# One transformer layer on one core: the gate weights stacked into one operand, and a head's values taken in one block of matmuls ahead of the next head's transposes

## What is computed

```python
proj = x @ w_in
qa, ka, va, qk_m, vm, om, gates = jnp.split(proj, SPLITS, axis=-1)
att = dilated_attention(heads(qa, 8), heads(ka, 8), heads(va, 8), rel_table)
...
ig = (gates[..., :4] + ig_b).transpose(0, 2, 1)      # 4 heads x 512
fg = (gates[..., 4:] + fg_b).transpose(0, 2, 1)
h = mlstm(heads(qm, 4), heads(km, 4), heads(vm, 4), ig, fg)
...
# memory_attention
kv = (mem @ wkv).reshape(B, L, 2, 4, 256)
k, v = kv[:, :, 0], kv[:, :, 1]
```

## Time and profile before

| | us |
|---|---|
| three runs | 1163.87, 1164.14, 1164.82 (median 1164.14) |
| the profiled execution | 1164.95 |
| its span in the trace | 1163.0 |
| PE busy | 1150.1 (99% of the span), 5490 matmuls |
| PE weight loads | 958.7 (82%) |
| DVE / ACT / POOL busy | 573.1 / 422.2 / 32.7 |
| granted PE clock | 0.999 of 2.4 GHz |

### The profile page before, as it was taken

One profiled execution on the slowest core, in us unless ns is written; L12 is line 12 of the kernel. 1 busy time (PEld: TensorE's weight loads), 2 busy tenths in 40 slices (PEclk: granted clock), 3 DMA queues, 4 the chain that ended last, 5 costly groups with the idle time before them and its releaser, 6 DMA issues.

```text
span 1163.0 us, 14755 instructions
## 1 busy us (share of the span) xinstructions
PE 1150.1 (99%) x5490; PEld 958.7 (82%) x5490; DVE 573.1 (49%) x930; ACT 422.2 (36%) x688; POOL 32.7 (3%) x49
## 2 busy tenths in 40 slices
PE   9999999999999999999999999999999999999997
PEld 8888888888888777888798888789888888888886
DVE  3533333343328588765884864456433333343325
ACT  4412212233225377643463454444221222233222
POOL 3000000000001011000000000000000000000000
PEclk9999999999999999999999999999999999999999
DMA  7532222232222222242243241232322222232211
GB/s 282 212 104 95 90 105 93 90 122 95 91 90 73 91 75 82 81 152 85 73 160 112 93 149 67 73 109 91 127 92 107 90 95 104 90 123 95 91 36 73
DMA packets 33563, 120.85 MB, mean 104 GB/s; under 512 B 3900, under 2 KB 3916, under 8 KB 33264
## 3 DMA queue, kind: packets, MB, share of 16 engines
q1 hardware_dynamic: 30528, 109.07, 27.3%
q0 software_dynamic: 2992, 11.19, 2.8%
HBM read 118.13 MB, written 2.11 MB: 103 GB/s over the span
## 4 chain that ended last, share of the span: by engine, by line
PE 97%; DVE 2%; ACT 1%; issue 0%; DVEq 0%; POOL 0%; POOLq 0%
PE ps L446 31%; PE ps L448 30%; PE ps L447 30%; PE ps L463 1%; PE ps L668 1%; PE ps L689 1%; PE ps L740 1%; PE ps L756 1%; PE ps L661 0%; PE ps L597 0%; PE ps L660 0%; DVE lg L1536 0%; PE ps L850 0%; DVE qs L1493 0%; DVE lg L1544 0%
## 5 line engine op out<-in xcount | busy, mean ns | idle before, releaser
L1336 DVE TENSOR_TENSOR wlo<-raw,whi 128x1024 fp32r<-128x1024 f32 x196 | 240.0, 1228 | 373.0 <-ACT whi L911 371.9
L446 PE MATMUL ps<-xth,whi 128*128 128x512 f32 (+1 forms) x924 | 355.0, 384 | 0.0
L448 PE MATMUL ps<-xth,wlo 128*128 128x512 f32 (+1 forms) x924 | 353.0, 382 | 0.0
L447 PE MATMUL ps<-xtl,whi 128*128 128x512 f32 (+1 forms) x924 | 352.9, 382 | 0.0
L911 ACT ACTIVATE whi<-raw 128x1024 fp32r<-128x1024 f32 (+1 forms) x204 | 207.1, 1037 | 152.1 <-PE ps L448 142.8
L448 PEld LDWEIGHTS ps<-xth,wlo 128*128 128x128 f32 x924 | 173.7, 188 | 34.1
L447 PEld LDWEIGHTS ps<-xtl,whi 128*128 128x128 f32 x924 | 173.8, 188 | 32.9
L446 PEld LDWEIGHTS ps<-xth,whi 128*128 128x128 f32 x924 | 173.8, 188 | 32.4
L446 PE MATMUL ps<-whi,hhi 128*128 128x512 f32 x480 | 187.8, 391 | 0.0
L448 PE MATMUL ps<-whi,hlo 128*128 128x512 f32 x480 | 186.9, 389 | 0.0
L447 PE MATMUL ps<-wlo,hhi 128*128 128x512 f32 x480 | 186.8, 389 | 0.0
(11 more groups left out here) (186 smaller groups left out, 997.2 us busy)
## 6 DMA issues: line engine op xcount, KB each, us to landing
raw<-in_units SPq DMA_DIRECT2D x204, 512.0 KB, 3.3
gb<-in_ln_g POOLq DMA_DIRECT2D x4, 512.0 KB, 3.9
gb<-in_ln_b POOLq DMA_DIRECT2D x4, 512.0 KB, 5.4
xn<-in_x POOLq DMA_DIRECT2D x4, 512.0 KB, 12.0
wb<-in_bias_by_key POOLq DMA_DIRECT2D x8, 256.0 KB, 3.0
out<-xn SPq DMA_DIRECT2D x8, 256.0 KB, 2.1
gsp<-g_rows POOLq DMA_DIRECT2D x1, 1024.0 KB, 4.8
memn<-in_mem_cols POOLq DMA_DIRECT2D x1, 1024.0 KB, 8.1
```

The costliest lines, as they stand in the source:

```text
L446: mm(dst, lh, rh, start=start, stop=False)
L447: mm(dst, lh, rl, start=False, stop=False)
L448: return mm(dst, ll, rh, start=False, stop=stop)
L1336: v.tensor_tensor(wlo[c % SPL][:, :], raw[c % RAW][:, :], whi[c % SPL][:, :].bitcast(F32), ALU.subtract).then_inc(lo_done, 1)
```

## The change

- The gate weights are one operand `wg` of 100 columns: high parts in columns 0 to 35, zeros, low parts in columns 64 to 99. Two matmuls for each slice (against the high and the low part of x) replace three; rows 64 and up of the result hold the products of the low weights. ACT copies two more blocks of 4x512 out (`r_e`, `r_a`), and DVE adds them where it added a bias alone. `wg` lies in the memory of `vx`, so POOL now fills `wg` with zeros at the start, and `vx` with ones once the gate rows are done.
- The probabilities of a whole head stand in `ph` and `pl`. `values(h)` is one block of 8 matmuls (512, 512, 384, 384, 256, 256, 128, 128 columns) in step 4h + 6, ahead of that step's transposes; the part in step 4h + 4 is gone.
- DVE writes the first two `kl` ahead of the split of weight unit `U_QK + 5`.
- `mem_key(0)` waits for the first half of `mtl`, and for the second after 12 matmuls.

```diff
             for k in range(KT):
-                last = three(ps[1][0:GW, :], wg_hi[:, k, :], wg_lo[:, k, :], xh[:, k, :], xl[:, k, :], k == 0, k == KT - 1)
+                mm(ps[1][0:64 + GW, :], wg[:, k, :], xh[:, k, :], start=k == 0, stop=False)
+                last = mm(ps[1][0:64 + GW, :], wg[:, k, :], xl[:, k, :], start=False, stop=k == KT - 1)
             last.then_inc(grow_ready, 1)
...
-            def values(h, part):
-
-                i0 = 2 * part
-                pe.wait_ge(p_lo_done, NB * h + i0 + 2)
...
+            def values(h):
+
+                pe.wait_ge(p_lo_done, NB * h + NB)
...
+                for j in range(NB):
+                    cols = slice(4 * j * P, (3 * j + NB) * P)
+                    for p in (ph, pl):
+                        last = mm(ps[4 + h % 2][:, j * P:], vs[j][:, h, :], p[:, cols],
+                                  start=j == 0 and p is ph, stop=j == NB - 1 and p is pl)
                 last.then_inc(pv_done, 1)
...
             def attention(n):
+                if n % NB == 2 and n > NB:
+                    values(n // NB - 1)
                 if 2 <= n < NA + 2:
                     transpose_p(n - 2)
                 if n < NA:
                     logits(n)
-                if n >= NB and n % 2 == 0:
-                    values(n // NB - 1, n // 2 % 2)
...
                 if t == 0:
-                    pe.wait_ge(mlo_done, 2)
                     pe.wait_ge(pj_ev, evacuated(G_C2 + 3))
...
-                cols_part(U_XK + t, ps[6 + t % 2][:, 0:MB * P], mth, mtl, 0, KT)
+                for half in range(2):
+                    if t == 0:
+                        pe.wait_ge(mlo_done, half + 1)
+                    cols_part(U_XK + t, ps[6 + t % 2][:, 0:MB * P], mth, mtl, 4 * half, 4 * half + 4)
...
             fn(r_f[:, :], ps[1][32:GW, :], ACT.Copy).then_inc(f_ready, 1)
+            fn(r_e[:, :], ps[1][96:64 + GW, :], ACT.Copy).then_inc(f_ready, 1)
+            fn(r_a[:, :], ps[1][64:64 + MH, :], ACT.Copy).then_inc(f_ready, 1)
...
-            split(U_QK + 5)
             k_lo(0, 0)
             k_lo(0, 1)
+            split(U_QK + 5)
```

More of the change, by code:

```diff
@@ L205, in macaron_layer @@
         pt = [at(f"pt{s}", [P, S], ar + (64 + 2 * s) * KB) for s in range(PTS)]
[L206 to L209, removed]
+        ph = at("ph", [P, 13 * P], ar + 64 * KB, F32R)
+        pl = at("pl", [P, 13 * P], ar + 64 * KB + 13 * P * 4, F32R)
         ob = [at(f"ob{s}", [P, NB, P], ar + (74 + 2 * s if s < 2 else 52 + 2 * s) * KB) for s in range(MH)]
@@ L213, in macaron_layer @@
         grow = at("grow", [MH, S], ar + 82 * KB + NB * MH * (P + 1) * 4)
-        wg_hi = at("wg_hi", [P, KT, GW], ar + 82 * KB + NB * MH * (P + 1) * 4, F32R)
-        wg_lo = at("wg_lo", [P, KT, GW], ar + 82 * KB + NB * MH * (P + 1) * 4 + KT * GW * 4, F32R)
+        wg = at("wg", [P, KT, 64 + GW], ar + 82 * KB, F32R)
         mth = at("mth", [P, KT, MB * P], ar + 32 * KB, F32R)
@@ L330, in transposed, with prob_blocks @@
         def transposed(n):
[L332 to L340, removed]
+            return ps[2 + n % 2][:, 0:(n % NB + 1) * P].rearrange("p (j c) -> p j c", c=P)
+        def prob_blocks(p, i):
+            return p[:, i * P:(4 * i + 1) * P].rearrange("p (j c) -> p j c", c=P)[:, 0:3 * i + 1:3, :]
         block = ctx.enter_context(nc.Block())
@@ L372, in _ @@
                                     base=0, pattern=[[-1, P]], channel_multiplier=1).then_inc(pool_ok, 1)
-            nc.gpsimd.memset(vx[:, :, :, :], 1.0).then_inc(pool_ok, 1)
+            nc.gpsimd.memset(wg[:, :, :].bitcast(F32), 0.0).then_inc(pool_ok, 1)
             pool.wait_ge(lo_done, KT - 2)
@@ L412, in _ @@
             bias_masked(1)
+            pool.wait_ge(grow_ready, 1)
+            nc.gpsimd.memset(vx[:, :, :, :], 1.0).then_inc(pool_ok, 1)
             pool.wait_ge(rows_done, 1)
@@ L426, in _ @@
                                     channel_multiplier=-1).then_inc(gdiag_done, 1)
-            pool.wait_ge(pv_done, 2 * AH)
+            pool.wait_ge(pv_done, AH)
             pool.dma_start(memn[:, :, :], mem_cols).then_inc(mem_in, 16)
@@ L670, in transpose_p @@
                 last.then_inc(tr_done, 1)
-            def values(h, part):
-                i0 = 2 * part
-                pe.wait_ge(p_lo_done, NB * h + i0 + 2)
-                if part == 0 and h == 1:
+            def values(h):
+                pe.wait_ge(p_lo_done, NB * h + NB)
+                if h == 1:
                     pe.wait_ge(acol_done, 1)
                     pe.wait_ge(emin_done, 1)
-                if part == 0 and h >= 2:
+                if h >= 2:
                     pe.wait_ge(att_out, h - 1)
[L681 to L689, removed]
+                for j in range(NB):
[3 more added lines that the diff above has]
+                                  start=j == 0 and p is ph, stop=j == NB - 1 and p is pl)
                 last.then_inc(pv_done, 1)
@@ L747, in numerators @@
                     pe.wait_ge(pj_ev, evacuated(G_VM + NB - 1))
-                    pe.wait_ge(pool_ok, 2)
+                    pe.wait_ge(pool_ok, 3)
                     pe.wait_ge(att_out, AH)
@@ L974, in ffn_up @@
                     act.wait_ge(small_in, 16 * SMALL)
-                    fn(wg_hi[:, :, :], wg_raw[:, :, :], ACT.Copy).then_inc(wg_hi_done, 1)
+                    act.wait_ge(pool_ok, 2)
+                    fn(wg[:, :, 0:GW], wg_raw[:, :, :], ACT.Copy).then_inc(wg_hi_done, 1)
                 with act.Fori(1, FT // 3) as i:
@@ L1111, in p_hi @@
                 act.wait_ge(tr_done, n + 1)
-                if i % 2 == 0 and h:
-                    act.wait_ge(pv_done, 2 * h - 1 + i // 2)
-                fn(prob_blocks(pah, pbh, i), transposed(n), ACT.Copy).then_inc(p_hi_done, 1)
+                if i == 0 and h:
+                    act.wait_ge(pv_done, h)
+                fn(prob_blocks(ph, i), transposed(n), ACT.Copy).then_inc(p_hi_done, 1)
             def part_copy(h):
                 t, e = divmod(h, 2)
-                act.wait_ge(pv_done, 2 * h + 2)
+                act.wait_ge(pv_done, h + 1)
                 fn(mt[1][half(e), t * S:(t + 1) * S], ps[4 + h % 2][half(1 - e), :], ACT.Copy).then_inc(part_done, 1)
@@ L1154, in om_block @@
                 evacuate(G_OM + b, om[:, b, :], *ready, func=ACT.Tanh, scale=0.5)
-            act.wait_ge(pool_ok, 2)
+            act.wait_ge(pool_ok, 3)
             vm_block(0)
@@ L1409, in ffn_up @@
                     dve.wait_ge(wg_hi_done, 1)
-                    v.tensor_tensor(wg_lo[:, :, :], wg_raw[:, :, :], wg_hi[:, :, :].bitcast(F32), ALU.subtract)\
+                    v.tensor_tensor(wg[:, :, 64:], wg_raw[:, :, :], wg[:, :, 0:GW].bitcast(F32), ALU.subtract)\
                         .then_inc(wg_done, 1)
@@ L1506, in _ @@
             split(U_QK + 4)
-            dve.wait_ge(f_ready, 1)
-            step.link(v.tensor_scalar(r_f[:, :], r_f[:, :], gbias[:, 1:2], None, ALU.add))
+            dve.wait_ge(f_ready, 2)
+            step.link(v.scalar_tensor_tensor(out=r_f[:, :], in0=r_f[:, :], scalar=gbias[:, 1:2], in1=r_e[:, :],
+                                             op0=ALU.add, op1=ALU.add))
             v.scalar_tensor_tensor(out=r_e[:, :], in0=r_f[:, :], scalar=-1.0, in1=r_f[:, :],
                                    op0=ALU.mult, op1=ALU.max).then_inc(fabs_done, 1)
-            v.tensor_scalar(r_ig[:, :], ps[1][0:MH, :], gbias[:, 0:1], None, ALU.add).then_inc(ig_done, 1)
+            dve.wait_ge(f_ready, 3)
+            v.scalar_tensor_tensor(out=r_ig[:, :], in0=ps[1][0:MH, :], scalar=gbias[:, 0:1], in1=r_a[:, :],
+                                   op0=ALU.add, op1=ALU.add).then_inc(ig_done, 1)
             q_lo(0)
@@ L1548, in p_lo @@
                 dve.wait_ge(p_hi_done, n + 1)
-                v.tensor_tensor(prob_blocks(pal, pbl, n % NB), transposed(n),
-                                prob_blocks(pah, pbh, n % NB).bitcast(F32), ALU.subtract).then_inc(p_lo_done, 1)
+                v.tensor_tensor(prob_blocks(pl, n % NB), transposed(n),
+                                prob_blocks(ph, n % NB).bitcast(F32), ALU.subtract).then_inc(p_lo_done, 1)
             def add_part(h):
@@ L1625, in weigh @@
                 if s < PTS:
-                    dve.wait_ge(pv_done, 2 * AH)
+                    dve.wait_ge(pv_done, AH)
                 else:
```

## The result

| | before | after |
|---|---|---|
| median, us (20 runs each) | 1163.95 | 1165.62 |
| lowest to highest | 1163.0 to 1164.82 | 1164.93 to 1166.42 |
| profiled execution / its span | 1164.95 / 1163.0 | 1165.65 / 1163.7 |

The ratio is 1.0014, 95% interval 1.0008 to 1.002: the change makes the kernel **1.7 us slower**. The forecast was 1163.5, 0.5 faster. The time lies in the range, the sign is wrong. The prediction took anything under 2.3 us for too small to tell; with 20 runs of each kernel, 1.7 us is told.

A forecast was written before the change was run, and what follows sets the result against it. PE was busy 99% of the span, with DVE nearly unbroken in the attention loop. Gates -1.85, first logits -0.30, loop +2.16 and memory's keys -0.62 gave -0.6 us: 1163.5 against the median, range 1160.9 to 1165.9.

The forecast's parts named there:

- Gates: Gate matmuls on PE: eight of 24 go, -1.85 us; ACT's two extra copies hide in its idle time, 0.
- First logits: Start of attention: `kl` ahead of DVE's weight split removes PE's 0.98 us wait; -0.30 us, ends 0 and -0.98.
- Memory's keys: Memory keys: first 12 matmuls start on `mtl`'s first half; gain limited by DVE before `numerators(3)`; -0.62 us, ends 0 and -1.1.
- What sets the loop's pace: Attention loop: DVE works nearly without a break, PE just behind; a shorter loop would show PE sets the pace.
- rival 1: PE is the bound after all; each loop boundary costs only its wait; -3.3 us, 1160.8, chance 0.18.
- Rival 2: First logits and memory keys give 0, loop boundaries cost a tenth more each; +1.0 us, 1165.1, chance 0.17.
- the loop's +2.16: Attention loop: sum of boundary shifts, part one of head 0 leaving, and old and new clashes; +2.16 us.
- The block's length: Values' block ahead of the transposes: 8 matmuls take 1.17 us, against 1.35 for the two parts before.
- The new clashes: Step 13: DVE's scaling meets POOL's mask add behind a query boundary and is stretched; +0.4 us.
- The old clash: Step 21: DVE's scaling, 1.11 us beside POOL's mask add, 0.29 elsewhere, gets clear of it; -0.75 us.
- Rival 3: POOL's add clashes with DVE's scaling in every head of the loop; +3.9 us, 1168.0, chance 0.09.
- The tests named: Trace signs listed beforehand, such as gate matmuls in 3.7 us, block waits about 0.3, and 7.8 us to step 9's transposes.

The follow-up runs named there:

- experiment 6: Against experiment 3: merged values' block moved behind the transposes and logits of step 4h + 6, with 10 matmuls in odd heads; 1160.85 us.
- experiment 8: Against experiment 3: DVE does `p_lo` of step 4h + 3 ahead of the bias and scaling of step 4h + 5; 1161.91 us.
- experiment 3: Against the changed kernel: POOL's mask add waits until DVE has scaled block 1 of the head before; 1164.35 us.
- experiment 12: Against the kernel before: only POOL's later mask add, the edit of experiment 3; 1163.58 us.
- base 4: Against the changed kernel: values as before (two parts, behind the logits) and POOL's later mask add; 1160.64 us.
- experiment 5: Against base 4: part two of the values (8 matmuls) ahead of the transposes of step 4h + 6; 1163.64 us.
- experiments 3 and 7: The second, 7, against experiment 6: merged block ahead of the transposes of step 4h + 7; 1160.39 us.

## Why the prediction was wrong, step by step

**Right.** *Gates*, -1.85: measured -1.8 alone. The copies did hide: ACT's three stand at 394.27 and its next split follows them. *First logits*, -0.30: gates, this and the part that leaves step 4 were to bring -2.61, and the traces show -2.60; transposes of step 4 wait 0.70 for the scaling, as forecast. *Memory's keys*, -0.62: the traces show -0.62, with `numerators(3)` behind DVE. *What sets the loop's pace*: a shift ahead of DVE's bias comes back at the transposes of step 4h + 5, because DVE has no break between; the loop grew, so rival 1 (PE is the bound) is out. At boundaries with queries PE's wait stands one step earlier, at the transposes of step 4h + 4 (437.80, 0.57 behind DVE's scaling), and those of step 13 (439.81) show none. Rival 2's 1165.1 came nearest to the measured time, but not by its mechanism, since both small gains hold in the traces.

**Wrong: the loop's +2.16.** For the same stretch as the measured 4.46 (without the 0.46 of part one of head 0) the sum gave 2.62. What failed are three of its terms.

1. *The block's length.* The 1.17 was the spacing of matmuls that follow each other undisturbed, and it left out what stands at the block's end: the last matmul is 0.11 ahead of what follows it, not 0.06, whatever that is. This 0.05 is in the 0.89 of the earlier trace rows, of which the sum took only 0.84. So even undisturbed, in experiment 6, the block takes 1.22. Where the change puts it, the first matmul waits, and its weights load only behind the wait: in after the PEld row starts with the matmul (421.44), in experiment 6 it starts 0.16 ahead (421.67, then 421.83). The second matmul follows 0.34 later instead of 0.23, and the block takes 1.34. Seven times 0.17: **+1.2**. Where the wait is gone, in experiment 8, the first two are still 0.27 to 0.31 apart; why, no run shows.
2. *The new clashes.* I had one, +0.4, in step 13. There were three, 0.42 in step 5, 0.43 in step 13 and 0.18 in step 21: 1.03 in the trace, and 1.27 by experiment 3. Step 13 came by the argument given: a query boundary moves the last bias more than the next scaling. I didn't carry the argument to step 5. There, part one (0.46 us) leaves step 4, between the bias that triggers the transfer for POOL and the scaling of step 5, and the two close in by just that. **+0.6**.
3. *The old clash.* Its end was counted at -0.75, against a profiled execution that held it. But the forecast was then set against the median, with the remark that this execution lay 0.8 above it. The clash may well be why it did. Against the median its going is worth about what experiment 12 gives, -0.5 by the medians and -0.2 by the ratio, and not told from 0. So 0.25 to 0.75 was counted twice. I take **+0.3**; no run fixes it.

-0.6 + 1.2 + 0.6 + 0.3 = +1.5, against the measured +1.67. The first two terms stand in the traces; the third is an estimate. By the boundaries, with the block's 0.17 and the measured clashes put in, the seven come to 1.16, 0.55, 1.17, 0.55, 0.10, 0.28 and 0.56, measured 1.12, 0.57, 1.17, 0.55, 0.18, 0.26 and 0.61.

**The sum's base.** The traces give +1.24 and the medians +1.67. Before's profiled execution had its 0.82 of clash in full. If the median run has some 0.46 of it (experiment 12's difference of medians, not told from 0), the traces come to 1.24 + 0.36 = 1.6. This step is a guess that fits. Nor does anything show why before was 0.59 behind where the gates start.

**Rival 3** (the clash in every head) had the right mechanism and too wide a reach: three heads of six, because at boundaries into the heads between add and scaling move nearly alike (from the add's start to the scaling's it was 1.52, 1.29 and 1.22 us before, and is 1.28, 1.37 and 1.24; into steps 5 and 13 it went from 1.20 and 1.18 to 0.67 and 0.65). The Trainium skill (SBUF — State Buffer, SBUF: two separate sides) lets a VectorE instruction in a two-port mode exclude GpSimd and be excluded by it. The trace agrees for the scaling, which where it is stretched ends 0.07 to 0.10 behind the add (420.79 after 420.70, 441.98 after 441.90, 462.92 after 462.85, before 463.29 after 463.19); in which mode it runs, no run shows. The bias of 256 columns, with one input in PSUM, ran beside the add at 440.72 in its usual 0.42.

**The tests named.** Right: 16 gate matmuls in 3.7 us, first logits without a wait, DVE idle ahead of its bias (0.94), block to transposes of step 9 in 7.95 us (7.8 said), wait of the transposes of step 4 (0.70), last numerators behind DVE. Half right: the blocks' waits, said to be about 0.3 at each; as lateness by start spacing it was 0.31 at four of seven, and 0.72, 0.74 and 0.48 where the scaling ahead was stretched. "I am wrong if scalings of 0.8 us and more stand in most heads": none did; the tests looked for the rivals, and had nothing for a block of 1.34.

**What stays open.** Merging saves 0.13 us a head of matmul spacing (1.22 against 1.35) where the block has 8 matmuls, 0.6 in all in experiment 6, and the time doesn't show it there. That the waits for DVE swallow it is likely (its transposes wait 1.9 us where base 4's wait 1.2), but no run isolates it. Nor does one separate the block's length from its place.

## What to carry to other kernels

Put ahead of a chain PE → DVE → PE, work delays the chain by its length and its wait, less the slack that the chain had, even when PE's own total falls; put where PE's next partner has slack, the same work is free. The same matmuls ahead or behind are 3.0 us apart in experiments 5 and 4, and the merged block 4.0 us in experiments 3 and 7. A block that is to start behind a wait costs more than its undisturbed spacing. When a forecast leans on a single profiled execution, take its chance events out of the base before counting their end as a gain, and for every removed piece ask which two other instructions it held apart.

## What the runs showed of the hardware

- A matmul of 512 columns whose wait ends late is 0.34 us ahead of the next one, against 0.23 in a row: its weight load starts at the same time as it (421.44), not under the matmul before it. It happens at each of the seven blocks of after (0.33 or 0.34). For 256 columns it is 0.22 or 0.23 against 0.12 (experiment 5, from 431.13 on).
- Beside POOL's add the scaling on DVE (0.29) stretched to anything between 0.47 and 1.15 in the rows shown here, and ended 0.07 to 0.10 us behind the add, wherever it began.
- POOL waited 2.3 to 2.6 us in most heads for a transfer of 256 KB, and 3.35, 3.39 and 4.18 in step 21 of three traces. With the later add no trace shows a stretched scaling, and after is 1.3 us faster.
